# w_down of each expert loaded through ScalarE's DMA queue instead of SyncE's

## The chip, the cores and the metric

The kernel runs on one core of a Trainium2 chip. The time is that of the device, in microseconds, for one execution; the value compared is the median of several.

## The reference, cut to what matters

The program is two blocks of a transformer on 256 tokens of width 1024, all in float32. The first (dilated attention beside an RWKV recurrence) and the mixer of the second (a long convolution beside differential attention) are not touched. What the change touches is the last part, a feed-forward layer in which each of 16 experts picks its own 32 tokens:

```
def _expert_choice_ffn(h, w_router, w_gate, w_up, w_down):
    ...
    g, idx = lax.top_k(aff.transpose(2, 0, 1), cap)
    xin = h[bi, idx]
    def expert(args):
        xe, wg, wu, wd = args
        a = jnp.einsum('bcd,df->bcf', xe, wg)
        u = jnp.einsum('bcd,df->bcf', xe, wu)
        return jnp.einsum('bcf,fd->bcd', jax.nn.silu(a) * u, wd)
    out = lax.map(expert, (xin, w_gate, w_up, w_down))
    out = out * g[..., None].astype(out.dtype)
    return jnp.zeros_like(h).at[bi, idx].add(out)
```

Here cap is 2 x 256 / 16 = 32 tokens, the width is 1024 and the hidden width 2816. Each expert thus reads three matrices of 1024 x 2816 float32 values, 34.6 MB, for only 32 tokens.

## The kernel before

Everything up to the experts takes the first 770 us. Each engine has its own instruction stream, and semaphores tie the streams together. In the last stage all of them run one loop over the 16 experts.

**Pieces and slots.** The weights of an expert are cut into 24 pieces of 128 partitions x 2816 float32 values (`PIECE`, 1.44 MB each). Pieces 0 to 7 are w_gate, 128 rows of it each, pieces 8 to 15 are w_up, and pieces 16 to 23 are w_down, laid out so that partition p holds rows 22p to 22p + 21. There are `SLOTS = 12` slots in SBUF; piece i goes to slot i mod 12. So piece 12 takes the place of piece 0, and pieces 0 to 11 of the next expert take the places of pieces 12 to 23. `arrived[slot]` is the semaphore on which a slot's landing is counted, `piece_used` the one by which PE says that it is through with a piece.

**SyncE** (L436 to L451) loads the first 12 pieces of the first expert while earlier work still runs. Then it goes through the pieces in the order in which PE wants them: before piece i it waits until piece i - 12 has been used (in the count of `piece_used`, e * 24 + i - 11), then issues the transfer. All of this is on SyncE's own hardware queue.

**PE** (L1203 to L1236) waits for `arrived` of a piece, multiplies the 32 gathered tokens with it (L1213: 8 matmuls of 352 columns in four column groups of the array; the profile records each float32 matmul as two, so 16 a piece) and signals `piece_used`. After piece 15 it waits for DVE, then runs the down projection over 22 rows per partition (L1227: 44 matmuls of 512 columns, also in four column groups; 88 records, 11 per piece on average; a piece is waited for when the first row needs it). Then it waits for ScalarE's copy and scatters the result to the tokens (L1235, 8 matmuls).

**ScalarE** (L710 to L716) has two instructions in the loop: the Exp of the gate (L713) when piece 7 has been used, and the copy of the expert's result (L716) when piece 23 has been used. **DVE** (L1678 to L1702) makes the sigmoid and the product with the gate (L1681 to L1686), waits for piece 15 to be used, multiplies with the up projection, repacks and transposes (L1689 to L1694), and adds the scattered results to the residual stream (L1699). GpSimd copies the next expert's tokens. After the loop come the last norm and the store of the output (L453).

Of the kernel before, what the change touches and what calls it, by code (L numbers as in the profile page):

```python
# [132 lines left out]
def program(nc, A, out):  # L133
    ctx = ExitStack()
    with ctx:
        def sem(name):
            return ctx.enter_context(nc.semaphore(name))
# [6 lines left out]
        def region(off, *shape):  # L144

            n = 1
            for s in shape:
                n *= s
            x = arena[:, off:off + n]
            if len(shape) == 2:  # L150
                x = x.rearrange("p (a b) -> p a b", a=shape[0])
            elif len(shape) == 3:
                x = x.rearrange("p (a b c) -> p a b c", a=shape[0], b=shape[1])
            elif len(shape) == 4:
                x = x.rearrange("p (a b c d) -> p a b c d", a=shape[0], b=shape[1], c=shape[2])
            return x
# [41 lines left out]
        def col(name, i=0, n=1):  # L198
            a = COLS[name][0] + i
            return cols[:, a:a + n]  # L200
# [75 lines left out]
        SLOTS = 12  # L276
# [5 lines left out]
        def slot(n):  # L282
            return region(PIECE * n, PIECE)
# [23 lines left out]
        S = {}  # L307
# [20 lines left out]
        arrived = [sem(f"piece{i}_in") for i in range(SLOTS)]  # L328
# [27 lines left out]
        blocks += [(f"at{i}", in_cols(A["w_in_2"], 1536 + 512 * i)) for i in range(3)]  # L356
        blocks += [(f"out2_{i}", in_cols(A["w_out_2"], 512 * i)) for i in range(2)]
        number = {name: n for n, (name, _) in enumerate(blocks)}

        def block_of(name):  # L360
# [10 lines left out]
        def piece(e, i):  # L371

            if i < 16:
                w = (wg if i < 8 else wu).rearrange("e k n -> (e k) n")
                return w[bass.ds(e * D + (i % 8) * P, P), :]
            return wd[bass.ds(e * P, P), (i - 16) * PIECE:(i - 15) * PIECE]
# [45 lines left out]
        @block.sync  # L422
        def _(sp):
            sp.dma_start(xres, A["x"].rearrange("(a p) d -> p a d", p=P)).then_inc(S["xin"], 16)
            sp.wait_ge(S["params"], 96)
            for n, (name, src) in enumerate(blocks):
                if n >= NB:
                    count, value = released[blocks[n - NB][0]]
                    sp.wait_ge(count, value)
                if name[0:2] == "up":  # L430
                    dst = wb_up[n % NB]
                else:
                    dst = wb[n % NB][:, :, 0:src.shape[2]]
                sp.dma_start(dst, src).then_inc(wload[n % NB], 16)

            used = S["x2_mm"]  # L436
            for i, count, value in ((5, S["z_done"], 1), (6, S["spec"], 2), (7, S["spec"], 2), (8, S["i_mm"], 2),
                                    (9, S["z_done"], 2), (10, S["hy_norm"], 1), (11, S["m_tr"], 2),
                                    (3, used, 3), (4, used, 3), (0, used, 4), (1, used, 4), (2, used, 4)):
                sp.wait_ge(count, value)  # L440
                sp.dma_start(slot(i), piece(0, i)).then_inc(arrived[i], 16)
            with sp.Fori(0, E - 1) as e:
                for i in range(SLOTS, 24):
                    sp.wait_ge(S["piece_used"], e * 24 + (i - 11))
                    sp.dma_start(slot(i - SLOTS), piece(e, i)).then_inc(arrived[i - SLOTS], 16)  # L445
                for i in range(SLOTS):
                    sp.wait_ge(S["piece_used"], e * 24 + (i + 13))
                    sp.dma_start(slot(i), piece(e + 1, i)).then_inc(arrived[i], 16)
            for i in range(SLOTS, 24):
                sp.wait_ge(S["piece_used"], (E - 1) * 24 + (i - 11))  # L450
                sp.dma_start(slot(i - SLOTS), piece(E - 1, i)).then_inc(arrived[i - SLOTS], 16)  # L451
            sp.wait_ge(S["out_ready"], 2)
            sp.dma_start(out.rearrange("(a p) d -> p a d", p=P), xres).then_inc(S["store"], 16)  # L453
            sp.wait_ge(S["store"], 16)
# [50 lines left out]
        def _(act):  # L505
# [200 lines left out]
            for k in range(KC):  # L706
                act.wait_ge(S["x_gather"], k + 1)
                dst = XE.rearrange("p (e k c) -> p e k c", e=E, k=KC)[:, :, k, :]
                act.activation(dst, psum[:, k % 4, :].rearrange("p (e c) -> p e c", e=E), ACT.Copy, scale=col("ffn_g", k)).then_inc(S["x_evac"], 1)
            with act.Fori(0, E) as e:  # L710
                act.wait_ge(S["piece_used"], e * 24 + 8)
                act.wait_ge(S["h_ready"], e + 1)
                act.activation(GE.rearrange("p (n x) -> p n x", n=2), psum[:, 0:2, 0:HALFQ], ACT.Exp, scale=-1.0).then_inc(S["g_expd"], 1)  # L713
                act.wait_ge(S["piece_used"], e * 24 + 24)
                act.wait_ge(S["acc_done"], e * 2 + 1)
                act.activation(YS, psum[:, 4:6, :], ACT.Copy).then_inc(S["y3_sb"], 1)  # L716
# [1026 lines left out]
```

## Time and profile before

| | us |
|---|---|
| median of 3 runs | 2057.76 |
| lowest and highest of them | 2056.74, 2058.26 |
| span of the profiled execution | 2056.9 |
| PE busy in it | 1579.2 |
| DVE busy in it | 529.1 |
| ScalarE busy in it | 162.9 |
| expert stage, first issue of the loop to the step of the last piece | 773.5 to 2037.8 |

The profile comes from one execution, whose own time is its span; nothing else of it is recorded. PE stands for TensorE's matmuls, PEld for its weight loads, SPq and ACTq for the instruction sequencers of SyncE and ScalarE, on which DMA issues are recorded with the time that they hold the sequencer. q1 is the hardware queue of SyncE, q10 that of ScalarE, q0 that of GpSimd. The granted clock (PEclk) is a share of TensorE's full clock of 2.4 GHz; 0.50 is 1.2 GHz.

### The profile page before, as it was taken

What the parts mean: (1) busy time and instruction counts of PE and PEld (TensorE: products, weight loads), DVE (VectorE), ACT (ScalarE), POOL (GpSimd) and SP (SyncE); (2) the same over time, 40 slices, a digit from 0 to 9 for tenths busy, and PEclk for the clock granted to TensorE, in tenths of its full rate; (3) what the DMA queues carried; (4) which work ended last, traced back from release to release, by engine and by line L of the source; (5) the groups of instructions that cost most, each with busy time, mean ns of one, the idle gap of its engine ahead of it and who ended that gap; (6) DMA issues with size and microseconds to landing.
All of it is one profiled execution on the core that took longest, in us unless ns stands there. A gap on an engine that the chain in (4) does not pass through costs nothing.

```text
span 2056.9 us, 22821 instructions
## 1 busy us (share of the span) xinstructions
PE 1579.2 (77%) x9754; PEld 745.6 (36%) x9754; DVE 529.1 (26%) x666; ACT 162.9 (8%) x318; POOL 25.2 (1%) x57
## 2 busy tenths in 40 slices
PE   8999998788999777766767666667677676676675
PEld 7857787674585342111111111111111111111111
DVE  1014577744534541111111111011111111010111
ACT  2112130010211220000000000000000000000000
POOL 0000000001000000000000000000000000000000
PEclk9999999779999989576675775766866757757667
DMA  8342221115133339999999999999999999999996
GB/s 311 134 169 83 82 82 43 42 57 184 41 123 123 156 140 403 425 426 425 426 425 425 426 425 426 425 426 425 425 426 425 426 425 425 426 425 426 425 425 273
DMA packets 89888, 629.13 MB, mean 306 GB/s; under 512 B 7242, under 2 KB 8365, under 8 KB 40628
## 3 DMA queue, kind: packets, MB, share of 16 engines
q1 hardware_dynamic: 87056, 619.21, 73.0%
q0 software_dynamic: 2224, 8.17, 1.2%
q10 hardware_dynamic: 564, 1.10, 0.1%
q8 instruction: 35, 0.57, 0.1%
q14 instruction: 9, 0.07, 0.0%
HBM read 627.37 MB, written 1.09 MB: 306 GB/s over the span
## 4 chain that ended last, share of the span: by engine, by line
DMA 43%; PE 35%; SPq 10%; DVE 8%; issue 2%; ACT 2%; DVEq 0%; POOL 0%; ACTq 0%; POOLq 0%
DMA arena<-in_w_down 15%; DMA arena<-in_w_up 14%; DMA arena<-in_w_gate 14%; PE psum L760 10%; SPq L445 9%; PE psum L1227 3%; PE psum L1213 3%; PE psum L1059 3%; PE psum L762 2%; PE psum L1235 1%; PE psum L983 1%; PE psum L886 1%; DVE arena L1371 1%; PE psum L779 1%; PE psum L1122 1%
## 5 line engine op out<-in xcount | busy, mean ns | idle before, releaser
L1213 PE MATMUL psum<-arena 128*32 128x352 f32 x4096 | 570.4, 703 | 201.6 <-DMA arena<-in_w_gate 100.7
L1227 PE MATMUL psum<-arena 128*32 128x512 f32 x1408 | 259.8, 683 | 165.1 <-DMA arena<-in_w_down 114.5
L1213 PEld LDWEIGHTS psum<-arena 128*32 128x32 f32 x4096 | 142.9, 145 | 622.0 <-DMA arena<-in_w_up 243.1
L760 PE MATMUL psum<-arena 128*128 128x256 f32 x976 | 225.3, 389 | 0.6 <-ACT arena L534 0.6
L1227 PEld LDWEIGHTS psum<-arena 128*32 128x32 f32 x1408 | 71.5, 121 | 357.5 <-DMA arena<-in_w_down 189.4
L760 PEld LDWEIGHTS psum<-arena 128*128 128x128 f32 x976 | 186.7, 194 | 31.2 <-issue 4.1
L1699 DVE TENSOR_TENSOR arena<-psum,arena 128x1024 f32<-128x1024 f32 x32 | 39.2, 1225 | 438.8 <-PE psum L1235 438.8
L1681 DVE TENSOR_SCALAR arena<-arena 128x704 f32<-128x704 f32 x16 | 8.4, 527 | 349.0 <-ACT arena L713 349.0
L1689 DVE TENSOR_TENSOR arena<-psum,arena 128x704 f32<-128x704 f32 x16 | 14.3, 892 | 306.5 <-PE psum L1213 306.5
L716 ACT ACTIVATE arena<-psum 128x1024 f32<-128x1024 f32 x16 | 16.4, 1024 | 830.4 <-PE psum L1227 830.4
L1235 PE MATMUL psum<-arena 128*128 128x512 f32 x128 | 59.2, 605 | 20.1 <-ACT arena L716 20.1
L1683 DVE RECIPROCAL arena<-arena 128x704 f32<-128x704 f32 x16 | 72.8, 4553 | 0.6
L1059 PE MATMUL psum<-arena 128*128 128x256 f32 x320 | 70.1, 379 | 1.5 <-DVE arena L1537 1.5
L1059 PEld LDWEIGHTS psum<-arena 128*128 128x128 f32 x320 | 60.6, 190 | 11.6 <-issue 3.6
L886 PE MATMUL psum<-arena 64*64 64x64 f32 x960 | 35.9, 241 | 14.3 <-DVE arena L1405 11.1
L1284 DVE TENSOR_TENSOR arena<-psum,arena 128x768 f32<-128x768 f32 (+1 forms) x16 | 12.1, 754 | 129.2 <-PE psum L779 129.1
L713 ACT ACTIVATE arena<-psum 128x704 f32<-128x704 f32 x16 | 12.1, 757 | 412.2 <-PE psum L1213 412.2
L1235 PEld LDWEIGHTS psum<-arena 128*128 128x128 f32 x128 | 23.0, 189 | 57.6 <-ACT arena L716 34.6
L762 PE MATMUL psum<-arena 128*128 128x512 f32 x96 | 41.4, 592 | 0.0
L886 PEld LDWEIGHTS psum<-arena 64*64 64x64 f32 x960 | 34.2, 155 | 17.9 <-DVE arena L1405 12.7
L532 ACT ACTIVATE arena<-psum 128x256 f32<-128x256 f32 (+1 forms) x51 | 20.9, 409 | 203.8 <-PE psum L760 165.9
L1122 PE MATMUL psum<-arena 128*128 128x512 f32 x64 | 32.3, 645 | 1.3 <-DVE arena L1621 1.3
(363 smaller groups left out, 1110.3 us busy)
## 6 DMA issues: line engine op xcount, KB each, us to landing
arena<-in_w_gate SPq DMA_DIRECT2D x128, 1408.0 KB, 35.1
arena<-in_w_up SPq DMA_DIRECT2D x128, 1408.0 KB, 35.3
arena<-in_w_down SPq DMA_DIRECT2D x128, 1408.0 KB, 35.6
arena<-in_w_in SPq DMA_DIRECT2D x24, 2048.0 KB, 8.2
arena<-in_w_out SPq DMA_DIRECT2D x4, 2048.0 KB, 7.8
arena<-bias_rows POOLq DMA_DIRECT2D x3, 1024.0 KB, 14.9
arena<-in_rows POOLq DMA_DIRECT2D x4, 512.0 KB, 10.3
arena<-in_w_up_attn SPq DMA_DIRECT2D x1, 2048.0 KB, 8.7
```

What stands on the lines that cost most here:

```text
L445: sp.dma_start(slot(i - SLOTS), piece(e, i)).then_inc(arrived[i - SLOTS], 16)
L532: act.activation(dst, src, ACT.Copy, scale=scale).then_inc(S["proj_evac"], 1)
L760: last = mm(o, block_of(blk)[:, k, c * P:c * P + P], rhs[:, k, :], start=(k == 0), stop=(k == KC - 1))
L762: last = mm(psum[:, j % 4, :], hR[:, k, c * P:c * P + P], block_of(blk)[:, k, :], start=(k == 0), stop=(k == KC - 1))
L886: last = mm(psum[p0:p0 + 64, bank + cp, i * CH:i * CH + CH], lhs[p0:p0 + 64, cp, i, :], rhs[p0:p0 + 64, cp, i, :], start=True, stop=True)
L1059: last = mm(psum[:, bank2_of(j), 0:T], block_of(name)[:, k, (j % 4) * P:(j % 4) * P + P], h2T[:, k, :], start=(k == 0), stop=(k == KC - 1))
L1122: last = mm(psum[:, i, :], mixT[:, k, a * P:a * P + P], block_of(name)[:, k, :], start=(k == 0), stop=(k == KC - 1))
L1213: last = mm(psum[32 * j:32 * j + CAP, b + n, 0:HALFQ], XC[:, k, :], w[:, c0:c0 + HALFQ], start=(k == 0), stop=(k == KC - 1))
L1227: last = mm(psum[32 * g:32 * g + CAP, 4 + n, :], HT[:, i, :], region(o, 512), start=(i < 4), stop=(i >= FPP - 4))
L1235: last = mm(psum[:, (6 if a == 0 else 4) + n, :], OC[:, a, :], YS[:, n, :], start=True, stop=True)
L1683: V.reciprocal(GE, GE).then_inc(S["dve_loop"], 1)
L1699: V.tensor_tensor(x, psum[:, b:b + 2, :], x, ALU.add).then_inc(S["acc_done"], 1)
```

## The change

The eight w_down transfers of each expert leave SyncE's stream and are issued by ScalarE, through ScalarE's own hardware queue. Three of them (pieces 16 to 18, which wait for pieces 4 to 6) stand ahead of the Exp, five (pieces 19 to 23, which wait for pieces 7 to 11) between the Exp and the copy. The waits before each transfer, the slots, the semaphores and everything on the other engines stay as they are.

```
@@ -440,13 +440,13 @@
             with sp.Fori(0, E - 1) as e:
-                for i in range(SLOTS, 24):
+                for i in range(SLOTS, 16):
                     sp.wait_ge(S["piece_used"], e * 24 + (i - 11))
                     sp.dma_start(slot(i - SLOTS), piece(e, i)).then_inc(arrived[i - SLOTS], 16)
                 for i in range(SLOTS):
                     sp.wait_ge(S["piece_used"], e * 24 + (i + 13))
                     sp.dma_start(slot(i), piece(e + 1, i)).then_inc(arrived[i], 16)
-            for i in range(SLOTS, 24):
+            for i in range(SLOTS, 16):
                 sp.wait_ge(S["piece_used"], (E - 1) * 24 + (i - 11))
                 sp.dma_start(slot(i - SLOTS), piece(E - 1, i)).then_inc(arrived[i - SLOTS], 16)
@@ -708,9 +708,15 @@
             with act.Fori(0, E) as e:
+                for i in range(16, 19):
+                    act.wait_ge(S["piece_used"], e * 24 + (i - 11))
+                    act.dma_start(slot(i - SLOTS), piece(e, i)).then_inc(arrived[i - SLOTS], 16)
                 act.wait_ge(S["piece_used"], e * 24 + 8)
                 act.wait_ge(S["h_ready"], e + 1)
                 act.activation(GE.rearrange("p (n x) -> p n x", n=2), psum[:, 0:2, 0:HALFQ], ACT.Exp, scale=-1.0).then_inc(S["g_expd"], 1)
+                for i in range(19, 24):
+                    act.wait_ge(S["piece_used"], e * 24 + (i - 11))
+                    act.dma_start(slot(i - SLOTS), piece(e, i)).then_inc(arrived[i - SLOTS], 16)
                 act.wait_ge(S["piece_used"], e * 24 + 24)
```

How the instructions stand on ScalarE in the loop over the experts, from the branch into it, before (arena is SBUF; ISA and REGISTER_ALU are a sequencer's waits and address arithmetic):

```order
L710 ISA
L712 REGISTER_ALU [waits piece_used]
L713 ACTIVATE arena<-psum 128x704 [waits h_ready]
L714 REGISTER_ALU
L715 ISA [waits piece_used]
L716 ACTIVATE arena<-psum 128x1024 [waits acc_done]
```

The same place after the change, from the third w_down issue to the second one behind the Exp:

```order
L713 DMA arena<-in_w_down 128x2816
L714 REGISTER_ALU
L715 REGISTER_ALU [waits piece_used]
L716 ACTIVATE arena<-psum 128x704 [waits h_ready]
L719 ISA [waits piece_used]
L719 DMA arena<-in_w_down 128x2816
```

The DMA rows are new on this engine: three ahead of the Exp (now L716), five behind it, each with its own wait for a used piece.

On SyncE, the end of the stream, where the last expert's pieces are issued after the loop:

```order
 L442 COMPARE_AND_BRANCH
 L451 DMA arena<-in_w_up 128x2816 [waits piece_used] x4
-L451 DMA arena<-in_w_down 128x2816 [waits piece_used] x8
 L453 DMA out<-arena 128x2x1024 [waits out_ready]
 L135 UNCONDITIONAL_BRANCH [waits store]
```

The eight w_down transfers are gone from it; the same eight are gone from the loop body, so that SyncE goes from piece 15 of an expert straight to piece 0 of the next.

## Rows read from the trace of the kernel before

**Rows 1.** The page: busy time; then 40 slices of the span, tenths and GB/s.
```profile
PE 1579.2 (77%) x9754; PEld 745.6 (36%) x9754; DVE 529.1 (26%) x666; ACT 162.9 (8%) x318; POOL 25.2 (1%) x57
...
DMA  8342221115133339999999999999999999999996
GB/s 311 134 169 83 82 82 43 42 57 184 41 123 123 156 140 403 425 426 425 426 425 425 426 425 426 425 426 425 425 426 425 426 425 425 426 425 426 425 425 273
```

**Rows 2.** Busy time, granted clock and DMA of a window: the expert stage.
```profile
core 0: us, PE busy (x) PEld busy (x) DVE busy (x) ACT busy (x) POOL busy (x), PEclk, DMA share, GB/s
773.50:2037.80 1264.30, 881.15 (x5597) 234.79 (x5589) 176.72 (x141) 27.48 (x31) 12.08 (x30) 0.70 1.01 424
```

**Rows 3.** Timeline of PE (start, us), w_down, then the next expert.
```profile
1214.49 1.92 PE L1227 MATMUL psum<-arena 128*32 128x512 f32 x8 [1.45 <-DMA arena<-in_w_down]
1217.89 1.93 PE L1227 MATMUL psum<-arena 128*32 128x512 f32 x12 [1.48 <-DMA arena<-in_w_down]
...
1224.66 1.94 PE L1227 MATMUL psum<-arena 128*32 128x512 f32 x12 [1.45 <-DMA arena<-in_w_down]
...
1231.48 2.57 PE L1213 MATMUL psum<-arena 128*32 128x352 f32 x32
...
1234.82 1.39 PE L1213 MATMUL psum<-arena 128*32 128x352 f32 x16 [0.77 <-DMA arena<-in_w_gate]
...
1268.70 2.57 PE L1213 MATMUL psum<-arena 128*32 128x352 f32 x16 [0.81 <-DMA arena<-in_w_up]
```

**Rows 4.** The page's DMA issues: count, KB each, median us to landing.
```profile
arena<-in_w_up SPq DMA_DIRECT2D x128, 1408.0 KB, 35.3
arena<-in_w_down SPq DMA_DIRECT2D x128, 1408.0 KB, 35.6
```

**Rows 5.** Timeline of the last expert, from piece 15 to the scatter.
```profile
2010.73 2.58 PE L1213 MATMUL psum<-arena 128*32 128x352 f32 x16 [0.81 <-DMA arena<-in_w_up]
...
2016.45 6.38 PE L1227 MATMUL psum<-arena 128*32 128x512 f32 x32 [3.15 <-DVE arena L1694]
...
2037.80 1.93 PE L1227 MATMUL psum<-arena 128*32 128x512 f32 x12 [1.41 <-DMA arena<-in_w_down]
...
2039.91 1.02 ACT L716 ACTIVATE arena<-psum 128x1024 f32<-128x1024 f32 x1 [52.81 <-PE psum L1227]
```

**Rows 6.** SyncE's issues of line L448 (ns, min/median/max), and three before the stage.
```profile
L448 SPq DMA_DIRECT2D arena<-in_w_gate x120: 332/2701/6733, 787.7 to 1947.2; - x120
...
657.11 1.58 SPq L441 DMA_DIRECT2D arena<-in_w_gate  x3
```

**Rows 7.** Timeline of the gate chain in one expert, and what DVE waits for.
```profile
1254.48 0.76 ACT L713 ACTIVATE arena<-psum 128x704 f32<-128x704 f32 x1 [26.68 <-PE psum L1213]
...
1260.42 0.89 DVE L1686 TENSOR_TENSOR arena<-psum,arena 128x704 f32<-128x704 f32 x1
...
1281.51 0.89 DVE L1689 TENSOR_TENSOR arena<-psum,arena 128x704 f32<-128x704 f32 x1 [20.20 <-PE psum L1213]
```

**Rows 8.** DMA queues over 3 to 4 us: packets, MB, share of 16 engines.
```profile
DMA packets 177, 0.40 MB, mean 401 GB/s; under 512 B 89, under 2 KB 89, under 8 KB 177
...
q1 hardware_dynamic: 88, 0.36, 88.5%
q10 hardware_dynamic: 89, 0.04, 14.4%
```

**Rows 9.** Timeline of weight loads in the last expert's down projection.
```profile
2017.28 0.42 PEld L1227 LDWEIGHTS psum<-arena 128*32 128x32 f32 x6 [0.64 <-issue]
2018.13 0.42 PEld L1227 LDWEIGHTS psum<-arena 128*32 128x32 f32 x4 [0.43 <-issue]
...
2021.35 0.14 PEld L1227 LDWEIGHTS psum<-arena 128*32 128x32 f32 x3 [0.29 <-issue]
2021.78 0.14 PEld L1227 LDWEIGHTS psum<-arena 128*32 128x32 f32 x3 [0.29 <-issue]
```

**Rows 10.** Windows as in rows 2: w_down piece, w_up piece, last expert's start.
```profile
1214.00:1217.00 3.00, 1.92 (x8) 0.40 (x8) 0.00 (x0) 0.00 (x0) 0.00 (x0) 1.00 1.01 424
...
1265.00:1269.00 4.00, 2.87 (x20) 0.79 (x24) 0.00 (x0) 0.00 (x0) 0.00 (x0) 0.50 1.02 428
...
2016.40:2023.00 6.60, 6.38 (x32) 2.16 (x32) 0.00 (x0) 0.00 (x0) 0.00 (x0) 0.71 1.01 427
```

**Rows 11.** DMA queues over 3 to 5 us, as in rows 8.
```profile
q1 hardware_dynamic: 187, 0.77, 93.5%
q10 hardware_dynamic: 131, 0.05, 9.8%
```

**Rows 12.** A window as in rows 2, before the stage, with one queue loaded.
```profile
663.00:669.00 6.00, 6.00 (x24) 2.95 (x23) 2.43 (x8) 0.60 (x1) 0.00 (x0) 1.00 1.05 433
```

More of the change, by code:

```diff
@@ L442, in _ @@
             with sp.Fori(0, E - 1) as e:
-                for i in range(SLOTS, 24):
+                for i in range(SLOTS, 16):
                     sp.wait_ge(S["piece_used"], e * 24 + (i - 11))
@@ L448, in _ @@
                     sp.dma_start(slot(i), piece(e + 1, i)).then_inc(arrived[i], 16)
-            for i in range(SLOTS, 24):
+            for i in range(SLOTS, 16):
                 sp.wait_ge(S["piece_used"], (E - 1) * 24 + (i - 11))
@@ L710, in _ @@
             with act.Fori(0, E) as e:
+                for i in range(16, 19):
+                    act.wait_ge(S["piece_used"], e * 24 + (i - 11))
+                    act.dma_start(slot(i - SLOTS), piece(e, i)).then_inc(arrived[i - SLOTS], 16)
                 act.wait_ge(S["piece_used"], e * 24 + 8)
@@ L713, in _ @@
                 act.activation(GE.rearrange("p (n x) -> p n x", n=2), psum[:, 0:2, 0:HALFQ], ACT.Exp, scale=-1.0).then_inc(S["g_expd"], 1)
+                for i in range(19, 24):
+                    act.wait_ge(S["piece_used"], e * 24 + (i - 11))
+                    act.dma_start(slot(i - SLOTS), piece(e, i)).then_inc(arrived[i - SLOTS], 16)
                 act.wait_ge(S["piece_used"], e * 24 + 24)
```

## The prediction

> **What bounds the kernel now.** I read the page first. PE is busy for 77% of the span, but the line of GB/s stands at 425 to 426 from slice 17 on, with the DMA digit at 9 [rows 1]. The window view of the expert stage, from the first issue that the loop makes (773.5 us) to the start of the last w_down step (2037.8 us), makes it exact: the 16 DMA engines busy at a share of 1.01 and 424 GB/s over 1264.3 us, while PE is busy for 881 of them [rows 2]. In that stretch SyncE's loop lands 384 - 12 = 372 pieces (the first 12 lie in SBUF before the stage), so one piece takes 1264.3 / 372 = 3.40 us; the w_down steps in the middle of the trace start 3.39 us apart and wait for the DMA each time [rows 3]. PE needs 2.57 us for a w_gate or w_up piece, or 1.29 to 1.39, and 1.9 us for a w_down piece [rows 3]. So every moment of this stage belongs to the DMA engines, and what the chain of waits calls SyncE's issue lies beside them: a piece takes 35 us from issue to landing [rows 4], which is ten others ahead of it.
>
> The end of the kernel is the one place that the DMA engines do not cover. Today the last piece to land is the last w_down piece; after it PE has only 12 recorded matmuls left (2037.80 to 2039.83), then the copy by ScalarE, the scatter and the final norm [rows 5]. The rest of the last expert's down projection had been done while the pieces came in.
>
> **The change part by part.** Number an expert's pieces 0 to 7 (w_gate), 8 to 15 (w_up), 16 to 23 (w_down); "used" means that PE is through with a piece.
>
> 1. Bytes, pieces, slots and matmuls stay the same. If the engines stay full, the time at which the last piece lands doesn't move, so nothing is gained in the stage: 0 us. SyncE loses 8 issues for each expert, some 2.7 us each (0.33 us where few transfers are in flight) [rows 6]. It was late by no more than what the depth of ten pieces hides, so this is 0 us too.
>
> 2. ScalarE gains 8 issues for each expert. Three stand ahead of its Exp, five ahead of its copy of the result. An issue took between 0.33 and 6.73 us on SyncE [rows 6]. Three at 6.73 us would put the Exp off by 20 us; behind it DVE's gate chain runs 6.8 us and then waits 20.2 us today for the last w_up piece [rows 7], and by step 3 that piece comes later still. The five others wait for pieces 7 to 11 to be used, long before the copy, which waits for piece 23. At the median of 2.7 us the Exp slips by a few us. Cost 0; if the cover were gone it would be the slip itself, in every expert.
>
> 3. The order of landing. This is where the sum comes from. Before, one queue held the pieces in the order in which PE wants them. Now piece 16 enters ScalarE's queue when piece 4 is used, while SyncE's queue still holds the pieces up to 15. The trace shows two hardware queues together only in its first microseconds: between 3 and 4 us, both loaded, SyncE's queue (q1) moved 88 packets and ScalarE's (q10) 89 [rows 8]. So I let two queues with equal packets share the engines by halves. The packets are the same rows of 11,264 bytes in both queues here. By the Trainium skill ("DMA: Bandwidth & Descriptors", Queues, rings and completion order) each DMA engine takes turns between its queues in units of about 9 to 17 descriptors, not row by row; by that unit the turns would be about a piece long, and the sum would shift by at most half a turn or so either way. The row on packets can't tell the two units apart.
>
> Walk through one expert, with T = 0 where piece 15 lands and the w_down pieces are in:
> - PE does piece 15 and the gate chain and starts the down projection 5.7 us later (2010.73 to 2016.45) [rows 5]. It needs no DMA now. 32 matmuls took 6.38 us when their pieces were there [rows 5], with weight loads 0.85 us apart at first and then 0.43 [rows 9]; the granted clock of that stretch is 0.71, between the level of 1.2 GHz (0.50) and that of 2.4 GHz (1.00) [rows 10]. The 56 others at the fast pace are 14 steps of 0.43 = 6.0 us: 12.4 us in all. Down done at 18.1.
> - 4.9 us on (copy and scatter: 1226.6 to 1231.5 between two experts [rows 3]) PE starts the next expert's piece 0, at 23.0. By then SyncE's queue, alone, has landed pieces 0 to 5. PE goes at 1.29 us each: piece 4 is used at 29.5. Now ScalarE's queue opens.
> - From here each queue gets a piece every 6.8 us. SyncE's piece 8 was nearly in and lands at 31.5; pieces 9 to 15 follow 6.8 us apart, the last at 79.0. ScalarE's 16 lands at 36.3, its 23 at 83.7, so that 2.35 us of transfer are left of it when piece 15 lands. 79 us for 23.3 pieces is the DMA engines' pace again: the pattern repeats itself, with the last w_down piece landing just behind the last w_up piece.
> - In the last expert no further pieces follow, so the rest of piece 23 runs alone and lands 2.35 us after piece 15. With the last landing at 2037.8, piece 15 lands at 2035.4, and the down projection ends at 2035.4 + 5.7 + 12.4 = 2053.5. Before it ended at 2039.8 [rows 5]. **+13.7 us**.
>
> Do the engines run dry anywhere? When piece 15 lands, SyncE's queue holds pieces 0, 1 and 2 of the next expert and gets piece 3 at 2.6: 13.6 us of work. The next (piece 4) enters when piece 16 is used, at about 7.5 us. Six us to spare, so no.
>
> Bounds of this term: if ScalarE's queue is served faster and piece 15 is the very last to land, 2.35 us more, +16.1; with the whole down projection at the slow pace (22 steps of 0.85 plus 0.65 = 19.4 us) 7 us more, +21 to +23. If w_down lags by four pieces, 13.6 us instead of 2.35 lie behind piece 15, and it is +2.5. I take the walk's value, since its one assumption is the nearest row (88 to 89).
>
> Sum: span 2056.9 + 13.7 = 2070.6. The median of the runs, 2057.8, is 0.9 above that span: 2071.5.
>
> **The rivals.**
> - *The engines serve the pieces in the order of issue all the same* (or ScalarE's issues come through so late or early that the order hardly changes). Then the last piece is still a w_down piece, with seven before it already used: 0 us, 2057.8. For it: today's single queue shows nothing that contradicts it. Against it: the 88 to 89. The Trainium skill (same page, "Issuing engines are not separate DMA queues") says that a second issuing engine only saves the sequencer's issue time; by that alone the time would stay where it is.
> - *w_down is starved and all slots fill up.* SyncE's queue needs 7.4 more pieces when ScalarE's opens. If ScalarE's gets only 3 parts in 10, it lands 7.4 x 0.3 / 0.7 = 3.2 pieces meanwhile (7.3 at even parts), and five are outstanding when piece 15 lands; PE waits for each, and each one that it uses lets SyncE load a piece of the next expert. When piece 23 lands all other slots are full. Then the engines stand for the 2.0 us of its matmuls, load one piece, and stand again until piece 0 is used (2.0 + 4.9 + 1.3 = 8.2, less 2.0 + 3.4): 2.0 + 2.8 = 4.8 us. For 15 experts 72 us: 2130. For it: over 3 to 5 us q10 moved 131 packets to q1's 187 [rows 11], though it may have had too little to send. Against: the even share while both are loaded.
> - *Two queues together move less* (or PE's pace in the tail is slow). 1% of the half of the stage in which both are loaded, 6 us, or 1% of the whole, 12.6 us: 2078 to 2084. The window with both queues shows 401 GB/s for small packets [rows 8], which neither supports nor excludes it.
> - *Faster.* The best window with one queue shows 433 GB/s [rows 12] against 424. Were two queues to hold that through the stage, 2.1% of 1264 us or 26 us would be gained, against 13.7 lost: 2046. It decides from a rate 1.1% higher. Against it: the share of 1.01 leaves no gap to fill.
>
> **How the numbers follow.** The walk: 0.66, 2071.5, its own range 2064 to 2081. Unchanged order: 0.14. Lower rate or slow tail: 0.06. Starved w_down: 0.09. Faster: 0.05. About 0.2% (4 us) is what a measurement of this kernel can tell from no change. The first and third and the starved case are slower, less a little where w_down lags by four pieces: 0.80. Same: the unchanged order and that little, 0.15. Faster: 0.05. The range from 2056.5 to 2085 holds the walk, the unchanged order and the lower rate, 0.86; it leaves out the starved case and the faster one.
>
> **What would show it.** In the changed kernel's profile: DMA still at 425 GB/s to within a piece of where it ended; q10 with some 184 MB; w_up steps of PE about 6.8 us apart (waits of some 4 us where they were 0.8), w_down matmuls with hardly a wait for the DMA; in the last expert the gap from the last L1213 matmul to the last of L1227 at about 15.5 us in place of 26.5, with the span ending later by 14 us. Wrong if w_up steps stay 3.4 us apart in the second half of an expert (order of issue), if the GB/s line dips at each expert (starved slots), or if it stands above 430.

## The result, and the profile after

| | before | changed |
|---|---|---|
| median, us | 2057.43 (4 runs) | 2073.07 (4 runs) |
| lowest and highest | 2056.74, 2058.26 | 2069.67, 2073.68 |
| ratio, 95% interval | | 1.0073 (1.006 to 1.0086) |
| span of the profiled execution | 2056.9 | 2071.0 |

The change makes the kernel slower by 15.0 us (12 to 18 by the interval; the medians are 15.6 apart); the forecast was 14 us slower, 2071.5. In the changed kernel the line numbers behind ScalarE's loop are 6 higher: L1219 is what was L1213 (w_gate and w_up), L1233 was L1227 (w_down), L1241 was L1235 (scatter).

The page of the changed kernel: busy time, then GB/s in 40 slices of the span, the queues (packets, MB, share of the 16 engines), and the issues with their median time to landing.

```profile
PE 1421.4 (69%) x9754; PEld 735.6 (36%) x9754; DVE 528.8 (26%) x666; ACT 162.9 (8%) x318; POOL 25.2 (1%) x57
...
GB/s 315 136 160 82 82 82 43 42 82 158 45 122 168 106 173 424 426 425 426 425 425 426 425 426 425 426 425 426 425 426 425 426 425 426 425 426 425 426 425 148
...
q1 hardware_dynamic: 68624, 434.65, 51.3%
q10 hardware_dynamic: 18996, 185.66, 21.3%
...
arena<-in_w_gate SPq DMA_DIRECT2D x128, 1408.0 KB, 16.3
arena<-in_w_up SPq DMA_DIRECT2D x128, 1408.0 KB, 32.8
arena<-in_w_down ACTq DMA_DIRECT2D x128, 1408.0 KB, 24.7
```

The rate in the stage is what it was in [rows 1]: 425 to 426. At its end the last slice differs, 148 where there were 273: the DMA engines are done and the kernel goes on. (The first slice of the stage has 424 where there were 403 because the slices of the longer span lie later: it begins at 776.6 us instead of 771.3.) w_gate now lands 16 us after its issue instead of 35.1, since no w_down piece stands ahead of it in SyncE's queue any more; w_up takes about as long as before [rows 4]. PE is busy for 158 us less though it runs the same matmuls. It has them in longer runs now, at a higher granted clock: 1.00 over the ten pieces from 1246.65 below (12.27 us), 0.50 at the single piece of 1264.30 (2.57 us). That buys nothing, since the stage waits for the DMA.

Timeline of PE in one expert in the middle, changed kernel (start, us, then what ended the idle time before):

```profile
1203.31 2.57 PE L1219 MATMUL psum<-arena 128*32 128x352 f32 x16 [4.20 <-DMA arena<-in_w_up]
...
1216.87 2.58 PE L1219 MATMUL psum<-arena 128*32 128x352 f32 x16 [4.21 <-DMA arena<-in_w_up]
1223.21 2.58 PE L1219 MATMUL psum<-arena 128*32 128x352 f32 x16 [3.77 <-DMA arena<-in_w_up]
1228.93 12.89 PE L1233 MATMUL psum<-arena 128*32 128x512 f32 x88 [3.14 <-DVE arena L1700]
1243.02 3.70 PE L1241 MATMUL psum<-arena 128*128 128x512 f32 x8 [1.20 <-ACT arena L722]
1246.65 12.27 PE L1219 MATMUL psum<-arena 128*32 128x352 f32 x160
1264.30 2.57 PE L1219 MATMUL psum<-arena 128*32 128x352 f32 x16 [5.38 <-DMA arena<-in_w_up]
```

In [rows 3] the steps are 3.39 us apart; here w_up pieces come every 6.78 us (the last one of the expert 6.34 us after the one before). Then all 88 matmuls of the down projection run in one piece, without a wait for the DMA, and so do ten pieces of the next expert. Over 13 us of that stretch the two queues of the changed kernel moved (window 1198 to 1211 us):

```profile
q1 hardware_dynamic: 278, 2.77, 50.6%
q10 hardware_dynamic: 277, 2.76, 50.3%
```

The end of the changed kernel, timeline of the last expert:

```profile
2028.37 2.58 PE L1219 MATMUL psum<-arena 128*32 128x352 f32 x16 [4.20 <-DMA arena<-in_w_up]
2035.13 2.58 PE L1219 MATMUL psum<-arena 128*32 128x352 f32 x16 [4.19 <-DMA arena<-in_w_up]
2037.78 0.89 DVE L1695 TENSOR_TENSOR arena<-psum,arena 128x704 f32<-128x704 f32 x1 [47.22 <-PE psum L1219]
...
2040.85 13.12 PE L1233 MATMUL psum<-arena 128*32 128x512 f32 x88 [3.14 <-DVE arena L1700]
2054.09 1.02 ACT L722 ACTIVATE arena<-psum 128x1024 f32<-128x1024 f32 x1 [69.60 <-PE psum L1233]
```

Compare with [rows 5]. There the last landing let PE start the last 12 matmuls at 2037.80 and ScalarE's copy stood at 2039.91, 2.1 us later. Here the landing of w_up piece 15 lets PE start that piece at 2035.13, and the copy stands at 2054.09, 19.0 us later: matmuls of that piece, gate product, repacking and transpose on DVE, and the whole down projection.

Piece 15 was not quite the last to land. The queues from 2033 to 2036 us:

```profile
q10 hardware_dynamic: 80, 0.72, 57.0%
q1 hardware_dynamic: 9, 0.03, 2.8%
```

ScalarE's queue still moved half a w_down piece while SyncE's had next to nothing left. In the packets of the trace, the last one of piece 15 ends at 2034.6 us, the last one of w_down at 2035.8. From that last packet to the copy it is 18.2 us; before, it was 2.7 (2037.2 to 2039.91). So 15.5 us more work stands behind the last byte.

### The profile page after: what moved, and what is told of

It is laid out like the page before. It is cut to its first block, busy times and chain, and to the rows that moved or that the text cites. A ratio compares the mean times of both kernels' runs of the same rounds, so it can differ in the third digit from the quotient of the medians.

```text
span 2071.0 us, 22831 instructions
## 1 busy us (share of the span) xinstructions
PE 1421.4 (69%) x9754; PEld 735.6 (36%) x9754; DVE 528.8 (26%) x666; ACT 162.9 (8%) x318; POOL 25.2 (1%) x57
## 4 chain that ended last, share of the span: by engine, by line
PE 48%; DMA 37%; DVE 9%; another core or an unknown queue 3%; ACT 2%; issue 1%; DVEq 0%; SPq 0%; ACTq 0%; POOL 0%; POOLq 0%
DMA arena<-in_w_up 32%; PE psum L766 10%; PE psum L1233 9%; PE psum L1219 7%; DMA arena<-in_w_down 5%; PE psum L1241 3%; PE psum L1065 3%; PE psum L768 2%; PE psum L989 1%; PE psum L892 1%; DVE arena L1377 1%; PE psum L785 1%; PE psum L1128 1%; PE psum L814 1%
## 5 line engine op out<-in xcount | busy, mean ns | idle before, releaser
L1219 PE MATMUL psum<-arena 128*32 128x352 f32 x4096 | 454.7, 597 | 466.6 <-DMA arena<-in_w_up 453.0
L1219 PEld LDWEIGHTS psum<-arena 128*32 128x32 f32 x4096 | 138.0, 129 | 775.6 <-DMA arena<-in_w_up 574.3
L1233 PE MATMUL psum<-arena 128*32 128x512 f32 x1408 | 215.9, 723 | 72.6 <-DVE arena L1700 50.3
L1233 PEld LDWEIGHTS psum<-arena 128*32 128x32 f32 x1408 | 66.6, 126 | 225.0 <-issue 193.0
L1241 PE MATMUL psum<-arena 128*128 128x512 f32 x128 | 62.6, 634 | 19.3 <-ACT arena L722 19.3
L1241 PEld LDWEIGHTS psum<-arena 128*128 128x128 f32 x128 | 24.3, 200 | 60.5 <-ACT arena L722 35.5
L892 PEld LDWEIGHTS psum<-arena 64*64 64x64 f32 x960 | 34.5, 156 | 18.3 <-DVE arena L1411 13.1
L716 ACT ACTIVATE arena<-psum 128x704 f32<-128x704 f32 x16 | 12.1, 757 | 231.0 <-PE psum L1219 231.0
```

The source lines that it names most:

```text
L892: last = mm(psum[p0:p0 + 64, bank + cp, i * CH:i * CH + CH], lhs[p0:p0 + 64, cp, i, :], rhs[p0:p0 + 64, cp, i, :], start=True, stop=True)
L1219: last = mm(psum[32 * j:32 * j + CAP, b + n, 0:HALFQ], XC[:, k, :], w[:, c0:c0 + HALFQ], start=(k == 0), stop=(k == KC - 1))
L1233: last = mm(psum[32 * g:32 * g + CAP, 4 + n, :], HT[:, i, :], region(o, 512), start=(i < 4), stop=(i >= FPP - 4))
L1241: last = mm(psum[:, (6 if a == 0 else 4) + n, :], OC[:, a, :], YS[:, n, :], start=True, stop=True)
```

## The experiments

Each was compared with the kernel before, run beside it on the same chip.

**Only the last expert's w_down goes back to SyncE.** Edit, against the changed kernel:

```
-            for i in range(SLOTS, 16):
+            for i in range(SLOTS, 24):
                 sp.wait_ge(S["piece_used"], (E - 1) * 24 + (i - 11))
...
-            with act.Fori(0, E) as e:
+            with act.Fori(0, E - 1) as e:
...
+            e = E - 1
+            act.wait_ge(S["piece_used"], e * 24 + 8)
+            act.wait_ge(S["h_ready"], e + 1)
...
+            act.wait_ge(S["piece_used"], e * 24 + 24)
+            act.wait_ge(S["acc_done"], e * 2 + 1)
...
```

> The w_down pieces of experts 0 to 14 go through ScalarE's queue as in the changed kernel; those of the last expert are issued by SyncE behind its w_up pieces. Theory (the whole loss is the last expert's order of landing, +16 us or so once, and nothing in the 15 experts before it): the last piece to land is w_down piece 23 again, the down projection ends some 2 us behind it, and the time is back at 2057.4, within 2 us. Rival (two queues cost something in every expert: some 1 us each, by a lower rate or by engines running dry): 14/15 of the loss stays, 2072 or so.

Measured: 2056.94 us against 2056.93, ratio 1.0001 (0.9991 to 1.0011). (The two times are medians. The ratio and its interval are estimated from all runs of both kernels, and in some of the experiments below they differ a little from the quotient of the medians.) The last expert's Exp and copy stand behind the loop, without transfers. With fifteen of sixteen experts on two queues, nothing of the loss is left. The page's queue rows and PE's timeline at the end:

```profile
q1 hardware_dynamic: 69776, 446.19, 53.0%
q10 hardware_dynamic: 17844, 174.12, 20.1%
```

```profile
2031.99 1.94 PE L1240 MATMUL psum<-arena 128*32 128x512 f32 x12 [1.46 <-DMA arena<-in_w_down]
2035.34 1.94 PE L1240 MATMUL psum<-arena 128*32 128x512 f32 x12 [1.42 <-DMA arena<-in_w_down]
2038.45 3.70 PE L1248 MATMUL psum<-arena 128*128 128x512 f32 x8 [1.18 <-ACT arena L729]
```

174 MB still went through ScalarE's queue, and the end reads like [rows 5]. A cost in every expert is excluded beyond 2.3 us in all, the upper end of the interval.

**Only the last expert's w_down goes to ScalarE.** Against the kernel before:

```
-            for i in range(SLOTS, 24):
+            for i in range(SLOTS, 16):
                 sp.wait_ge(S["piece_used"], (E - 1) * 24 + (i - 11))
...
-            with act.Fori(0, E) as e:
+            with act.Fori(0, E - 1) as e:
...
+            e = E - 1
+            for i in range(16, 19):
+                act.wait_ge(S["piece_used"], e * 24 + (i - 11))
+                act.dma_start(slot(i - SLOTS), piece(e, i)).then_inc(arrived[i - SLOTS], 16)
...
+            for i in range(19, 24):
+                act.wait_ge(S["piece_used"], e * 24 + (i - 11))
+                act.dma_start(slot(i - SLOTS), piece(e, i)).then_inc(arrived[i - SLOTS], 16)
...
```

> The reverse: SyncE issues everything for experts 0 to 14, ScalarE issues w_down for the last expert alone. Theory: when piece 4 of the last expert is used, SyncE's queue holds pieces 5 to 15; at even parts the eight w_down pieces land beside 5 to 12, and 13, 14 and 15 land alone, so piece 15 is the very last. Then 5.7 us to the start of the down projection and 12.4 to 13.1 us for it, against 2.0 us in the kernel before: +16.1 to +16.8, 2073.5 to 2074.2, no less than the whole change. Rival (a cost in every expert): one sixteenth of it, about 1 us, 2058.4.

Measured: 2072.26 against 2056.93, ratio 1.0079 (1.0062 to 1.0096), that is 15 us by the medians and 16 by the ratio. One expert in sixteen gives the whole loss. PE's timeline at its end:

```profile
2025.98 2.58 PE L1226 MATMUL psum<-arena 128*32 128x352 f32 x16 [4.20 <-DMA arena<-in_w_up]
2032.36 2.58 PE L1226 MATMUL psum<-arena 128*32 128x352 f32 x16 [3.80 <-DMA arena<-in_w_up]
2035.71 2.57 PE L1226 MATMUL psum<-arena 128*32 128x352 f32 x16 [0.78 <-DMA arena<-in_w_up]
2041.43 12.04 PE L1240 MATMUL psum<-arena 128*32 128x512 f32 x88 [3.15 <-DVE arena L1707]
```

The spacing tells the order of landing: 6.8 us while ScalarE's queue was loaded (6.4 from 2025.98 to 2032.36, where it ran out), then 3.35 us for the last piece (2032.36 to 2035.71), which landed alone, after w_down was complete.

**w_up through ScalarE instead of w_down.** SyncE keeps pieces 0 to 7 and 16 to 23; ScalarE issues 12 to 15 ahead of the Exp and 8 to 11 of the next expert around the copy:

```
-                for i in range(SLOTS, 24):
+                for i in range(16, 24):
...
-                for i in range(SLOTS):
+                for i in range(8):
...
+                for i in range(12, 16):
+                    act.wait_ge(S["piece_used"], e * 24 + (i - 11))
+                    act.dma_start(slot(i - SLOTS), piece(e, i)).then_inc(arrived[i - SLOTS], 16)
...
+                for i in range(8, 11):
+                    act.wait_ge(S["piece_used"], e * 24 + (i + 13))
+                    act.dma_start(slot(i), piece(e + 1, i)).then_inc(arrived[i], 16)
```

> Another third moves: ScalarE issues the eight w_up pieces of each expert, SyncE those of w_gate and w_down (the first twelve pieces of the first expert stay with SyncE). As many bytes go through the second queue as in the changed kernel. Theory (what costs is which piece lands last): w_down pieces 20 to 23 are now the last in SyncE's own queue, piece 23 lands last, and the last expert ends as in the kernel before: 2057.4, within 2 us. Rival (the second queue, or the issues on ScalarE, cost by themselves): 2070 or more, as in the changed kernel.

Measured: 2058.07 against 2057.06, ratio 1.0001 (0.9987 to 1.0015). Nearly as many transfers on ScalarE (124 for 128), nearly as many bytes in the second queue (180 MB on q10, where the changed kernel has 186), no loss: 3.1 us at most, by the interval. PE at the end:

```profile
2010.50 13.04 PE L1232 MATMUL psum<-arena 128*32 128x352 f32 x144 [4.19 <-DMA arena<-in_w_gate]
2026.70 7.13 PE L1246 MATMUL psum<-arena 128*32 128x512 f32 x64 [3.16 <-DVE arena L1713]
...
2037.55 1.93 PE L1246 MATMUL psum<-arena 128*32 128x512 f32 x12 [1.41 <-DMA arena<-in_w_down]
```

It is w_gate that comes at half pace here. Nine pieces then run at once (x144), because w_up had come ahead of its turn, and the last to land is a w_down piece, with 1.93 us of matmuls behind it. So it isn't the second queue that costs, but which piece it leaves for last.

**Odd pieces through ScalarE, even ones through SyncE.** Ranges with a step of 2 on both engines, the waits unchanged:

```
-                for i in range(SLOTS, 24):
+                for i in range(SLOTS, 24, 2):
...
+                for i in range(13, 19, 2):
+                    act.wait_ge(S["piece_used"], e * 24 + (i - 11))
+                    act.dma_start(slot(i - SLOTS), piece(e, i)).then_inc(arrived[i - SLOTS], 16)
```

> Pieces with odd numbers are issued by ScalarE, those with even numbers by SyncE, all at the same used pieces as before, so both queues are loaded through the whole stage and the order of landing stays in pairs. Theory: pieces 22 and 23 of the last expert land together, PE has 22 recorded matmuls left instead of 12, 3.0 us instead of 1.9: +1.1, 2058.5. Rival (two queues loaded together move less): 1% less would be 12.6 us here, since both are loaded all the time: 2070.

Measured: 2059.57 against 2057.06, ratio 1.0002 (0.9989 to 1.0015). The medians are 2.5 us apart, the ratio makes 0.4 us of it and 3.1 at most, so the 1.1 us can't be told from nothing. But a rate 1% lower with both queues loaded all the time (12.6 us) is excluded. The window 790 to 2030 us of this kernel (PE, PEld, DVE, ACT, POOL busy; PEclk; DMA share; GB/s):

```profile
790.00:2030.00 1240.00, 780.59 (x5348) 248.90 (x5348) 170.74 (x138) 26.70 (x30) 12.02 (x30) 0.79 1.01 426
```

**Only pieces 20 to 23 through ScalarE.** Against the kernel before:

```
-                for i in range(SLOTS, 24):
+                for i in range(SLOTS, 20):
...
+                for i in range(20, 24):
+                    act.wait_ge(S["piece_used"], e * 24 + (i - 11))
+                    act.dma_start(slot(i - SLOTS), piece(e, i)).then_inc(arrived[i - SLOTS], 16)
```

> Only pieces 20 to 23 of each expert go through ScalarE's queue, 16 to 19 stay with SyncE behind w_up. Theory: pieces 20 to 23 land beside 9 to 12, and piece 19 is the last to land; then PE has the matmuls of pieces 19 to 23 left, 55 records or 14 steps of 0.43 plus 0.65 = 6.6 us against 1.9: +4.6, 2062.0. The gate chain is hidden again, so the loss is a third of that of the changed kernel, not half of it (2065.2), which a cost in proportion to the diverted bytes would give.

Measured: 2063.96 against 2057.06, ratio 1.0028 (1.0016 to 1.004), 5.8 us with an interval of 3.3 to 8.2 (6.9 by the medians). The expected 4.6 lies inside; half the loss of the change (7.8) does too, so the ratio alone doesn't decide. The timeline does:

```profile
2030.03 6.38 PE L1230 MATMUL psum<-arena 128*32 128x512 f32 x32 [3.15 <-DVE arena L1697]
2037.83 7.08 PE L1230 MATMUL psum<-arena 128*32 128x512 f32 x56 [1.42 <-DMA arena<-in_w_down]
2046.11 3.70 PE L1238 MATMUL psum<-arena 128*128 128x512 f32 x8 [1.20 <-ACT arena L719]
```

The last piece to land starts 56 matmuls at 2037.83, the place where 12 stood before: 7.08 us instead of 1.93, +5.1, and this profile's span is 5.1 us above that of before (2062.0).

**Half rows on ScalarE.** Each w_down piece as two transfers of half its columns, both through ScalarE:

```
+        def half(eng, e, i, h):
+            w = wd[bass.ds(e * P, P), (i - 16) * PIECE + h * (PIECE // 2):(i - 16) * PIECE + (h + 1) * (PIECE // 2)]
+            eng.dma_start(region(PIECE * (i - SLOTS) + h * (PIECE // 2), PIECE // 2), w).then_inc(arrived[i - SLOTS], 16)
...
-                    act.dma_start(slot(i - SLOTS), piece(e, i)).then_inc(arrived[i - SLOTS], 16)
+                    half(act, e, i, 0)
+                    half(act, e, i, 1)
```

> As the changed kernel, but each w_down piece is sent as two transfers of half its columns (rows of 5,632 bytes instead of 11,264), both through ScalarE's queue. If the DMA engines take turns by rows or by transfers, ScalarE's queue now gets one part in three of the bytes. While SyncE lands its 7.4 pieces up to piece 15, ScalarE lands 3.7 instead of 7.3; the other four land after it, each one that PE uses lets SyncE load a piece of the next expert, and when piece 23 lands all other slots are full: the engines stand for 4.8 us in each of 15 experts, about 72 us, with dips in the GB/s line: 2120 to 2130. If the turns go by bytes, nothing changes against the changed kernel: 2073.

**Its control: the same half rows, all through SyncE** (the function above, called in SyncE's loops; one queue, order as before).

> Control for the half rows: as the kernel before (all by SyncE, one queue), but each w_down piece as two transfers of half its columns. Theory: rows of 5,632 bytes move as fast as those of 11,264 and the order stays, so 2057.4 within 2 us. If the smaller rows cost themselves, what this kernel loses has to be taken off the kernel with half rows on ScalarE's queue.

Measured: the control 2065.22, ratio 1.0042 (1.0028 to 1.0056); half rows on ScalarE 2118.56, ratio 1.0296 (1.0274 to 1.0318). The control was expected to cost nothing and costs 8 us (6 to 12 by the interval): its rate in the window 790 to 2030 us is 422 GB/s where that of the kernel before is 426. The row of the control, then that of the kernel with half rows on ScalarE:

```profile
790.00:2030.00 1240.00, 867.19 (x5314) 224.59 (x5315) 170.66 (x138) 26.70 (x30) 12.02 (x30) 0.69 1.01 422
790.00:2030.00 1240.00, 749.78 (x5012) 214.85 (x5012) 159.53 (x129) 24.94 (x28) 11.68 (x29) 0.69 0.98 405
```

Taken off, 53 us are left for the two queues (2118.56 less 2065.22), where 72 was worked out. The first half of the mechanism, the shares of the queues, is as expected. Queues of the kernel with half rows on ScalarE, window 1557 to 1561 us, both loaded:

```profile
q1 hardware_dynamic: 115, 1.12, 66.2%
q10 hardware_dynamic: 117, 0.57, 35.2%
```

The counts stay even while the bytes are 2 to 1. So the engines take turns by count, not by bytes. (Rows and transfers were both halved here; that the turn is one row is read from the trace of the changed kernel, under "Even parts" below.) The second half, engines that run dry, is there too. The same kernel at the end of one expert, in windows (last two columns: DMA share, GB/s):

```profile
1532.00:1534.00 2.00, 1.61 (x6) 0.42 (x9) 0.00 (x0) 0.00 (x0) 0.00 (x0) 0.50 1.01 428
1534.00:1536.00 2.00, 2.00 (x9) 0.21 (x3) 0.00 (x0) 0.00 (x0) 0.00 (x0) 0.50 0.15 62
1536.00:1538.00 2.00, 0.75 (x4) 0.50 (x2) 0.00 (x0) 1.02 (x1) 0.00 (x0) 0.50 0.55 141
...
1544.00:1546.00 2.00, 2.00 (x32) 0.89 (x28) 0.41 (x2) 0.00 (x0) 0.00 (x0) 1.00 0.52 135
1546.00:1548.00 2.00, 2.00 (x32) 0.91 (x28) 0.00 (x0) 0.00 (x0) 0.00 (x0) 1.00 0.80 315
```

All slots are full, and the DMA engines stand for about 1.7 + 0.9 us while PE does the last w_down piece, and for 1.0 + 0.4 us until the next expert's pieces give slots back: 4.0 us, against 4.8. SyncE had two pieces to load between the two stops, not one. This expert is one of the worst. Counted from the packets of the trace, in steps of 0.1 us, eleven of the fifteen rounds have such stops, of 2.3 to 4.3 us, and four have none: 36 us in all, against 2 in the control. The other 17 of the 53 us are a lower rate while the engines work: SyncE's rows of 11,264 bytes took 436 ns each in this kernel and 427 in the control. Why they are slower beside rows of half the size was not tried. This rival of the forecast is real, then, at half its price, and lies one row size away from the change as made.

## Why the prediction was right

**The bound, and the pieces' rate.** Right: 424 GB/s in [rows 2], 425 to 426 after, and a share of 1.01 in both. The kernel with odd and even pieces apart shows the same with both queues loaded throughout. The rival that two queues move less is excluded for rows of equal size, and so is the faster one.

**ScalarE's eight issues.** Right that they cost nothing, and for a stronger reason than given. They were bounded by SyncE's 0.33 to 6.73 us [rows 6]; they took 0.34, the five behind the Exp as follows (ns, min/median/max):

```profile
L719 ACTq DMA_DIRECT2D arena<-in_w_down x80: 339/339/340, 780.5 to 2010.8; - x80
```

DVE's product with the up projection, which waited 20.2 us in [rows 7], waited 47.2 us in the last expert, so the cover had grown as said.

**Even parts.** Right: 278 packets to 277. [Rows 8] had been enough for it, and what [rows 11] seemed to say against it was only a queue that had too little to send: of its 131 packets q10 moved 2 in the last half microsecond, when q1 moved 52.

The prediction left open whether a turn is one row or about a piece long. The changed kernel's trace tells. ScalarE's queue joins at 1256.5 us, with all engines in step; the windows 1256.9 to 1257.3 and 1257.3 to 1257.7 us:

```profile
q1 hardware_dynamic: 15, 0.16, 93.5%
q10 hardware_dynamic: 2, 0.02, 13.4%
...
q10 hardware_dynamic: 14, 0.16, 93.4%
q1 hardware_dynamic: 2, 0.02, 13.4%
```

A row takes 0.43 us on its engine, and after one row the engines change over to the other queue. A turn as long as a piece would be 3.4 us, so the longer unit that the prediction quotes is not seen here.

The rule of the Trainium skill ("DMA: Bandwidth & Descriptors", Issuing engines are not separate DMA queues), that a second issuing engine only saves the time of issue, holds here for the rate; the time did not stay where it was, because the order of landing changed.

**The walk.** Its steps stand in the timeline above, counted from piece 15 at 1223.2: down projection at +5.7 (forecast 5.7), next expert at +23.4 (23.0), w_up pieces 6.78 us apart (6.8). One step failed: "the pattern repeats itself". ScalarE's first issue came at 1252.98, at +29.8 where the walk has 29.5, but the walk let its rows flow from the issue on. They began 3.5 us later, at 1256.48, and SyncE's queue had the engines alone until then: piece 10 was there at +41.1, where the walk has 45.1. In the last expert it was 3.4 us (issue at 1979.90, first row at 1983.33). In between, from 1979.9 to 1983.3 us, q10 moved nothing and q1 one piece:

```profile
q1 hardware_dynamic: 145, 1.45, 101.4%
```

So SyncE's queue has less left than the walk says when the two begin to share: piece 15 lands sooner, and w_down behind it. The starts of piece 15 in the seventh to the tenth expert (the sixth is the one at 1223.21 above):

```profile
1298.19 2.57 PE L1219 MATMUL psum<-arena 128*32 128x352 f32 x16 [4.20 <-DMA arena<-in_w_up]
...
1385.87 2.58 PE L1219 MATMUL psum<-arena 128*32 128x352 f32 x16 [4.21 <-DMA arena<-in_w_up]
...
1461.68 2.58 PE L1219 MATMUL psum<-arena 128*32 128x352 f32 x16 [4.20 <-DMA arena<-in_w_up]
...
1547.23 2.58 PE L1219 MATMUL psum<-arena 128*32 128x352 f32 x16 [4.20 <-DMA arena<-in_w_up]
```

75.0, 87.7, 75.8 and 85.6 us apart: two experts take 163 us, each alone does not take 81. In the sixth expert both queues end together (piece 15 at 1222.6, w_down at 1222.7). In the seventh, piece 15 lands at 1297.6 and w_down only at 1310.6, 13 us behind it; SyncE's queue has to share for these 13 us at the start of the eighth, and there both end together again. The last interval is 85.1 us: the sixteenth expert is of the kind whose queues end nearly together.

**The size of the tail.** The walk left 2.35 us of piece 23 behind piece 15; it was about 1.3 us (2034.6 to 2035.8), which makes the loss 1.1 us larger. The down projection took 13.1 us where the walk has 12.4, with a granted clock of 0.57 over its first 6 us and 1.00 behind them: 0.7 us more. With both, 13.7 becomes 15.5 us, and that is what the ends of the two timelines give (18.2 less 2.7). The medians differ by 15.6. The two spans differ by 14.1 only because the stage of the changed kernel began 1.4 us earlier in its profiled execution (SyncE's first issue at 772.19, before at 773.55), in a part that the change doesn't touch; from the first packet of the loop to the last the DMA engines worked 1262.7 us in both. So the forecast difference was 1.9 us short of the medians', with both parts found. (The forecast time, 2071.5, also rests on adding 0.9 us to a span, a median of runs less the span of another execution; in the changed kernel the profiled run's own time is 1.8 above its span.)

What was luck is the kind of the last expert. The walk had all experts alike, and they aren't. If the last one had been of the seventh's kind, w_down would have landed some 13 us behind piece 15 instead of 1.3, and by the walk's own sum the loss would have been about 4 us (15.5 + 1.3 - 13). That is an estimate; no kernel with another number of experts was run. That the loss lies in the last expert's order of landing isn't luck, as the kernels with one expert each way show.

**Starved w_down** was given 0.09 and did not happen at rows of equal size. Where it did happen, with half rows, its price of 4.8 us in each of fifteen rounds was twice what it cost: 4.3 us in the worst round, none in four of them, 36 us in all where 72 were worked out.

## What to carry to other kernels

In a stage that is bound by transfers, as here, moving some of them to another queue gained nothing in rate, but it changed the order in which data lands; ask which transfer lands last and how much work stands behind it, since only the end of the stage shows it. Divert the operand that is needed early (w_up here, no loss), or bring the last iteration back into one queue (no loss either), rather than the one that is used last. And if two queues share the engines, give them rows of like size: the one with the smaller rows gets fewer bytes, and with a fixed number of slots that can starve the consumer and then the engines. When every iteration has the same instructions, still read more than one: here two kinds took turns, and which one came last set the loss.

## What the runs showed of the hardware that was not expected

**A deep queue holds its sequencer.** SyncE's issues took 2.7 us at the median in the kernel before [rows 6]. In the changed kernel the same instruction takes 0.33 us every time, the DMA engines being just as busy:

```profile
L448 SPq DMA_DIRECT2D arena<-in_w_gate x120: 332/333/336, 786.4 to 1964.3; - x120
```

In the kernel with odd and even pieces apart, where each queue holds about half of the outstanding pieces and a transfer still takes 38 us to land, SyncE's issues of w_down:

```profile
L445 SPq DMA_DIRECT2D arena<-in_w_down x60: 332/333/333, 778.0 to 1916.9; - x60
```

So it is what waits in one queue that holds the engine (some ten pieces of 128 rows held it, half as many didn't), not the load of the DMA engines. Whether transfers, rows or bytes count was not told apart. On SyncE it cost nothing. On an engine that also computes, 2.7 us for each issue could count; no run here shows that.

**A queue that joins waits one piece.** With the engines busy for SyncE's queue, the first row of ScalarE's came 3.4 to 3.5 us after its issue in the seven places that were read (six in the changed kernel, one in the kernel with only the last expert's w_down on ScalarE), the time of one piece of 128 rows. With the engines idle at the start of the stage, SyncE's first row came 1.0 us after its issue (773.55 to 774.5).

**Half rows cost up to one percent.** A third of the bytes in rows of 5,632 bytes instead of 11,264, with twice as many transfers, took the stage from 426 to 422 GB/s; the time rose by 8 us. Whether it is the rows or the number of transfers was not tried.
